# Projections of the first stage: modulation and sample products in four strips, modulation between the projection blocks

## The reference, cut to what matters

```python
mod = (silu(c) @ w_ada + b_ada).reshape(b, 6, d)      # c: 1 prompt row, 8 sample rows; w_ada: 1024 x 6144
sh1, sc1, g1, sh2, sc2, g2 = ...                      # six slices of 1024 columns
hmix = rms_norm(x) * (1.0 + sc1) + sh1
proj = hmix @ w_in                                    # w_in: 1024 x 3072
q, k, v, hc, gb, gc = split(proj)                     # six blocks of 512 columns
q, k = rotary(q), rotary(k)
u = gc * hc ; yconv = gb * conv3(u)                   # gated short convolution
```

## Time and profile before

| | |
|---|---|
| executions | 1468.34, 1470.19, 1476.89 us |
| the profiled execution: time | 1473.47 us |
| its span in the trace | 1471.6 us |
| mean granted clock of TensorE | 0.923 |
| TensorE busy | 1329.9 us (90%) |
| VectorE, ScalarE, GpSimd busy | 463.1, 204.7, 146.4 us |
| DMA | 354.26 MB, mean 241 GB/s |

### The profile page before, as it was taken

One profiled execution on the slowest core, in us unless ns is written; L12 is line 12 of the kernel. 1 busy time (PEld: TensorE's weight loads), 2 busy tenths in 40 slices (PEclk: granted clock), 3 DMA queues, 4 the chain that ended last, 5 costly groups with the idle time before them and its releaser, 6 DMA issues. The chain is left out here.

```text
span 1471.6 us, 19665 instructions
## 1 busy us (share of the span) xinstructions
PE 1329.9 (90%) x5999; PEld 576.9 (39%) x5999; DVE 463.1 (31%) x1185; ACT 204.7 (14%) x410; POOL 146.4 (10%) x152
## 2 busy tenths in 40 slices
PE   4999999988996669988999999899999999899495
PEld 1225554436674424443333333333333333333132
DVE  0340313203333224466233332233233233233248
ACT  0000010003222111111111111111111111111100
POOL 1000000000000010010111111111111111111121
PEclk9999999995558789999999999999999999999868
DMA  9990210019305875004999799989989779967375
GB/s 322 381 318 23 67 49 0 0 41 296 99 0 152 249 250 202 29 4 199 357 382 370 291 372 421 421 307 381 369 340 405 297 307 405 378 246 276 99 312 212
DMA packets 75065, 354.26 MB, mean 241 GB/s; under 512 B 11595, under 2 KB 11595, under 8 KB 44823
## 3 DMA queue, kind: packets, MB, share of 16 engines
q1 hardware_dynamic: 57166, 308.90, 55.8%
q0 software_dynamic: 15680, 37.05, 6.6%
q10 hardware_dynamic: 2130, 7.39, 1.4%
HBM read 338.54 MB, written 34.21 MB: 253 GB/s over the span
## 5 line engine op out<-in xcount | busy, mean ns | idle before, releaser
L1001 PE MATMUL psum<-sb_stream,sb_convg 128*64 128x512 f32 x1664 | 376.8, 606 | 22.7 <-DMA sb_stream<-w_exp_up 21.2
L1001 PEld LDWEIGHTS psum<-sb_stream,sb_convg 128*64 128x64 f32 x1664 | 120.1, 140 | 235.8 <-issue 234.4
L1027 PE MATMUL psum<-sb_stream,sb_aT 128*64 128x512 f32 x832 | 190.0, 598 | 0.0
L1132 POOL DMA_INDIRECT expert_rows<-sb_attn,sb_row x52 | 52.2, 1005 | 542.2 <-DVE sb_token L961 285.0
L500 PE MATMUL psum<-sb_stream,sb_hT 128*128 128x512 f32 (+1 forms) x240 | 105.5, 600 | 0.0
L472 PE MATMUL psum<-sb_hT,sb_stream 128*128 128x512 f32 x192 | 103.9, 634 | 0.6 <-DVE sb_hT L359 0.6
L439 PE MATMUL psum<-sb_stream,sb_cT 128*9 128x512 f32 x192 | 85.3, 608 | 11.5 <-DMA sb_stream<-w_ada 11.5
L1419 DVE TENSOR_TENSOR sb_aT<-psum,sb_aT 128x256 f32<-128x256 f32 x53 | 22.5, 425 | 228.7 <-ACT sb_aT L1205 228.7
L1027 PEld LDWEIGHTS psum<-sb_stream,sb_aT 128*64 128x64 f32 x832 | 55.1, 136 | 95.4 <-issue 89.3
L1447 DVE TENSOR_SCALAR sb_attn<-psum,sb_now_gate 128x512 f32<-128x512 f32 x52 | 39.0, 751 | 148.9 <-PE psum L1027 148.9
L1205 ACT ACTIVATE sb_aT<-psum 128x256 f32<-128x256 f32 x53 | 20.3, 383 | 388.1 <-PE psum L1001 386.7
(11 more groups left out here) (271 smaller groups left out, 1221.8 us busy)
## 6 DMA issues: line engine op xcount, KB each, us to landing
sb_stream<-w_exp_gate SPq DMA_DIRECT2D x65, 1024.0 KB, 7.3
sb_stream<-w_exp_up SPq DMA_DIRECT2D x65, 1024.0 KB, 10.3
sb_stream<-w_exp_down SPq DMA_DIRECT2D x65, 1024.0 KB, 10.3
sb_stream<-w_ada SPq DMA_DIRECT2D x12, 2048.0 KB, 11.9
sb_stream<-expert_rows SPq DMA_DIRECT2D x8, 2048.0 KB, 13.0
sb_stream<-w_in SPq DMA_DIRECT2D x6, 2048.0 KB, 7.9
sb_stream<-cache_k SPq DMA_DIRECT2D x8, 1024.0 KB, 18.5
sb_stream<-cache_v SPq DMA_DIRECT2D x8, 1024.0 KB, 13.3
```

The costliest lines, as they stand in the source:

```text
L1001: last = pe.matmul(psum[lo:lo + LANE, 0, :].rearrange("p (a n) -> p a n", a=2), xT[:, k, lo:lo + LANE], gu[j][:, k, :, :], start=(k == 0), ...
L1027: last = pe.matmul(psum[lo:lo + LANE, 4 + n, :], hidT[:, k, lo:lo + LANE], dn[j][:, k, n * 512:(n + 1) * 512], start=(k == 0), stop=(k == 1))
L1132: pool.indirect_dma_start(expert_rows, bass.IndirectOffsetOnAxis(ap=row[:, u, :], axis=0), out[:, u, :], None, bounds_check=last_expert_ro ...
```

## The change

- **Modulation in strips.** silu(c) is filled up to 32 columns with zeros. A piece of w_ada is now a *slab*: 256 rows of the contraction by 2048 columns (2 MB). Its 8 matmuls write four strips of 32 partitions of one bank: strip j has columns 512j to 512j+511 of the slab. Twelve slabs, four for each third of w_ada; each third has a bank of its own, in which its sums build up. The first third is shift and scale.
- **Order.** Only slabs 0 to 3 stand ahead of the projections; 4 to 6 stand behind the first convolution block, 7 to 9 behind the second, 10 and 11 behind the third. SyncE loads x first, then slabs 0 to 3, three blocks of w_in and so on; slabs and blocks have rings of three slots each.
- **Shift and scale on turned rows.** ScalarE only multiplies x by its norm (`normalize`); TensorE turns x; then scale and shift, turned too by four transposes, are applied to `hT`, where they are one number for each partition: four pieces by VectorE, four by ScalarE. The trip of shift and scale through DRAM is gone.
- **Sample rows in four strips of the contraction.** The 32 sample rows are stationary (128 x 32), 512 columns of w_in move, and the eight pieces of the contraction are spread over four strips, two in each. ScalarE copies the four partial sums out of PSUM, and a matmul with a matrix of four identities under each other (`fold`) adds them up: turned (4 matmuls) for the convolution blocks, as rows (1 matmul) for q, k, v. VectorE's convolution of the sample rows takes all four column tiles at once.

The core of the diff:

```diff
-        bc_shift = tmp("bc_shift", [P, 2, D])
-        bc_scale = tmp("bc_scale", [P, 2, D])
...
+        mod = tmp("mod", [P, 3, W])
+        modT = tmp("modT", [P, 2, KC, 1 + DEC_B])
+        part = tmp("part", [P, W])
+        side = tmp("side", [P, 2, W])
+        product = tmp("product", [P, WC, NS])
...
+        slots = stream[:, :].rearrange("p (s n) -> p s n", s=6)
+        slab = slots[:, 0:3, :].rearrange("p s (k n) -> p s k n", k=2)
+        ring = slots[:, 3:6, :].rearrange("p s (k n) -> p s k n", k=KC)
...
+        ada_bank = (1, 2, 7)
...
+                def load_slab(n):
+                    if n >= 3:
+                        sp.wait_ge(slab_used, n - 2)
+                    s, u = n // 4, n % 4
+                    src = io["w_ada"][0][2 * u * P:2 * (u + 1) * P, s * 4 * W:(s + 1) * 4 * W]
+                    sp.dma_start(slab[:, n % 3], src.rearrange("(k p) n -> p k n", p=P)).then_inc(slab_in[n % 3], 16)
+                def load_block(j):
+                    if j >= 3:
+                        sp.wait_ge(cmm, WC * (j - 2))
+                    src = io["w_in"][0][:, order[j] * W:(order[j] + 1) * W]
+                    sp.dma_start(ring[:, j % 3], src.rearrange("(k p) n -> p k n", p=P)).then_inc(w_in[j % 3], 16)
...
+                sp.dma_start(xh[:, 0:NPT, :], io["x_prompt"][0].rearrange("(t p) n -> p t n", p=P)).then_inc(x_in, 16)
+                sp.dma_start(xh[0:NS, NPT, :], io["x_sample"].rearrange("b t n -> (b t) n")).then_inc(x_in, 16)
+                for n in range(4):
+                    load_slab(n)
+                for j in range(3):
+                    load_block(j)
+                for n in range(4, 8):
+                    load_slab(n)
+                load_block(3)
+                for n in range(8, 11):
+                    load_slab(n)
+                load_block(4)
+                load_slab(11)
+                load_block(5)
...
+                def normalize(t):
+                    r = rows(t)
+                    act.activation(xh[0:r, t, :], xh[0:r, t, :], ACT.Copy, scale=ss[0:r, 0, t:t + 1]).then_inc(h_ok, 1)
...
+                act.wait_ge(mt_ok, 1)
+                for k in range(1, KC, 2):
+                    act.activation(hT[:, k, 0:SEQ], hT[:, k, 0:SEQ], ACT.Identity, bias=modT[:, 0, k, 0:1],
+                                   scale=modT[:, 1, k, 0:1]).then_inc(hT_a, 1)
...
+                    act.wait_ge(part_ps, j + 1)
+                    if j:
+                        act.wait_ge(merged, j)
+                    act.copy(part[:, :], psum[:, 5, :]).then_inc(part_ok, 1)
...
+                take_hc(0)
+                take_part(0)
+                take_hc(1)
+                act.wait_ge(merged, 1)
+                act.copy(hcT[:, :, SEQ:], psum[:, 6, 0:WC * NS].rearrange("p (c n) -> p c n", c=WC)).then_inc(merge_read, 1)
+                take_hc(2)
+                take_hc(3)
+                take_part(1)
+                keep_mod(1)
+                take_part(2)
...
+                def add_bias(s):
+                    v.wait_ge(slab_used, 4 * s + 4)
+                    v.tensor_tensor(mod[:, s, :], psum[:, ada_bank[s], :], mod[:, s, :], ALU.add).then_inc(mod_ok, 1)
...
+                def modulate(k):
+                    v.tensor_scalar(hT[:, k, 0:SEQ], hT[:, k, 0:SEQ], modT[:, 1, k, 0:1], modT[:, 0, k, 0:1],
+                                    ALU.mult, ALU.add).then_inc(hT_v, 1)
...
+                step(v.tensor_tensor(us[:, :, :, 2:], merge, hcs, ALU.mult))
...
-                for n in range(NADA):
-                    pe.wait_ge(w_in[n % 4], 16 * (n // 4 + 1))
-                    if n >= 2:
-                        pe.wait_ge(mod_ok, n - 1)
-                    for k in range(KC):
-                        last = pe.matmul(psum[0:9, 1 + n % 2, :], cT[:, k, :], ring[:, n % 4, k, :],
-                                         start=(k == 0), stop=(k == KC - 1))
-                    last.then_inc(w_used, 1)
...
+                def modulation(slabs):
+                    for n in slabs:
+                        s, u = n // 4, n % 4
+                        pe.wait_ge(slab_in[n % 3], 16 * (n // 3 + 1))
+                        for k in (2 * u, 2 * u + 1):
+                            for j in range(4):
+                                last = pe.matmul(psum[32 * j:32 * (j + 1), ada_bank[s], :], cT[:, k, :],
+                                                 slab[:, n % 3, k % 2, j * W:(j + 1) * W], start=(k == 0), stop=(k == KC - 1))
+                        last.then_inc(slab_used, 1)
...
+                def sample_strips(j):
+                    if j:
+                        pe.wait_ge(part_ok, j)
+                    else:
+                        pe.wait_ge(hT_v, NT + KC // 2 + 1)
+                    for i in range(2):
+                        for a in range(4):
+                            k = 2 * a + i
+                            last = pe.matmul(psum[32 * a:32 * (a + 1), 5, :], hT[:, k, SEQ:], ring[:, j % 3, k, :],
+                                             start=(i == 0), stop=(i == 1))
+                    last.then_inc(part_ps, 1)
...
+                def merge_turned(j):
+                    pe.wait_ge(part_ok, j + 1)
+                    if j:
+                        pe.wait_ge(merge_read, j)
+                    for c in range(WC):
+                        last = pe.matmul(psum[:, 6, c * NS:(c + 1) * NS], part[:, c * P:(c + 1) * P], fold, start=True, stop=True)
+                    last.then_inc(merged, 1)
...
+                    pe.matmul(psum[0:NS, 6, :], fold, part[:, :], start=True, stop=True).then_inc(merged, 1)
...
+                def conv_block(j):
+                    pe.wait_ge(w_in[j % 3], 16 * (j // 3 + 1))
+                    for m in range(WC):
+                        i = j * WC + m
+                        if i >= 2:
+                            if i - 2 < WC:
+                                pe.wait_ge(hc_ok, i - 1)
+                            else:
+                                pe.wait_ge(gcb_ok, i - 1 - WC)
+                        for k in range(KC):
+                            if i == 0:
+                                pe.wait_ge((hT_v, hT_a)[k % 2], NT + k // 2 + 1)
+                            last = pe.matmul(psum[:, 3 + i % 2, :], ring[:, j % 3, k, m * P:(m + 1) * P], hT[:, k, 0:SEQ],
+                                             start=(k == 0), stop=(k == KC - 1))
+                        last.then_inc(cmm, 1)
+                        if m == 0:
+                            sample_strips(j)
+                        if m == 1:
+                            merge_turned(j)
...
+                modulation((0, 1))
...
+                modulation((2, 3))
+                pe.wait_ge(small_in, 7 * 16)
+                for m in range(WC):
+                    last = pe.transpose(psum[:, 7, 16 * m:16 * m + 16], state[:, m * P:(m + 1) * P], ident[0:16, 0:16])
+                last.then_inc(turned, 1)
+                pe.wait_ge(mod_ok, 1)
+                for c in range(4):
+                    last = pe.transpose(psum[:, 0, c * P:(c + 1) * P], mod[:, 0, c * P:(c + 1) * P], ident)
+                last.then_inc(turned, 1)
+                conv_block(0)
+                modulation((4, 5, 6))
+                conv_block(1)
+                modulation((7,))
+                pe.wait_ge(st_ok, 1)
+                modulation((8, 9))
+                conv_block(2)
+                modulation((10, 11))
...
-                            last = pe.matmul(psum[:, 5 + i % 2, 0:NS], ring[:, n % 4, k, m * P:(m + 1) * P], hT[:, k, SEQ:],
-                                             start=(k == 0), stop=(k == KC - 1))
...
+                            last = pe.matmul(psum[:, i % 3, :], hT[:, k, t * P:(t + 1) * P], ring[:, n % 3, k, :],
                                              start=(k == 0), stop=(k == KC - 1))
                         last.then_inc(proj, 1)
+                        if t == 0:
+                            sample_strips(n)
+                        if t == 1:
+                            merge_rows(n)
```

More of the change, by code:

```diff
@@ L234, in _ @@
                 sp.dma_start(cst[:, :], io["cst"]).then_inc(cst_in, 16)
[L235 to L244, removed]
+                sp.dma_start(xh[:, 0:NPT, :], io["x_prompt"][0].rearrange("(t p) n -> p t n", p=P)).then_inc(x_in, 16)
[12 more added lines that the diff above has]
+                load_block(5)
+                sp.wait_ge(qk_ok, 2 * NPT)
                 sp.wait_ge(v_ok, NT)
+                sp.wait_ge(merge_read, 5)
                 for name, src in (("k", k_sb), ("v", v_sb)):
@@ L300, in _, with take_v @@
                     act.activation(convg[:, m, :], convT[:, m, :], ACT.Copy, scale=gains[:, 1, m:m + 1]).then_inc(sq_ok, 1)
-                act.wait_ge(pads, 1)
-                for t in range(NT):
-                    act.wait_ge(proj, 2 * NT + t + 1)
-                    act.copy(v_sb[0:rows(t), t, :], psum[0:rows(t), (2 * NT + t) % 3, :]).then_inc(v_ok, 1)
```

(42 more changed lines are left out.)

262 lines of the change are left out of this document (129 added, 133 removed).

## The result

Four executions of the changed kernel took 1399.79 to 1407.87 us, median 1402.12, beside four of the kernel before with a median of 1469.99: ratio 0.9536 (95% interval 0.9491 to 0.958). Two later series of six against eleven gave 0.9492 (0.9451 to 0.9533) and 0.9517 (0.9487 to 0.9547). The kernel is about 5% faster. The forecast was 1391 (1377 to 1409).

The account below looks back on a forecast made before the run. TensorE's count of matmuls was taken to bound stage 1; head 46 us plus the work behind it gave 247.5 against 326.2, 78.7 less, so 1391 us from the median 1470.19, range 1377 to 1409.

Parts of the forecast that it names:

- Head: Stage 1 up to the first projection: 43.5 us, plus 2.5 for a first 5 us at half clock, 46 together.
- Strips: Stage 1 matmuls on TensorE: four strips of 32 columns run in the time of one, 0.858 us a round.
- return: TensorE going from strips back to the full array in stage 1: 0.15 us each time.
- Cover: Stage 1 behind the first projection: VectorE, ScalarE and load waits cost nothing, hidden behind TensorE's tiles; some 27 us of load slack.
- rivals on the clock: Clock falls to half behind the first projection: about 1592 us, 3 in 100. Stage 2 gets better clock: 1346 to 1376, 4.
- strips that don't overlap: Stage 1: strips don't run beside each other, a round costs 3.43 us, the kernel takes 1475; 3 in 100.
- the tiles: Stage 1 projections: 12 tiles of the convolution and 12 of q, k, v at 6.87 us, 164.9 us, unchanged.
- the upper bound: Whole kernel at 1406 us: 6.5 more before the first projection, 5.9 for rounds at 1.07, 2 for entries into strips.
- folds and slabs: Stage 1 behind the first projection: folds 2.6 and 3.0 us; slabs 4 to 11, 16 rounds and five returns, 14.5.
- the sums of squares: Stage 1, with the tail ahead of k: 4.15 and 0.5 us, as before.
- what is passed on: Stages 2 to 4 behind the barrier: as long as before, so stage 1's saving of 78.7 us is passed on whole.
- The base: Whole kernel: the saving was taken from the median before, 1470.19 us; the profiled execution took 1473.47.

Follow-up runs that it names:

- c0_changed: The changed kernel timed again without any edit, beside the kernel before: median 1401.01 us against 1475.11, ratio 0.9492.
- the early stores: Changed kernel, but SyncE stores the convolution's state and k as soon as ready, only v's stores behind v's last copy: median 1401.74 us against 1404.8, ratio 0.9505.

## Why the prediction was right, and where it was short

The mechanism was right in each of its parts, and experiments show the two large ones.

- *Head.* Forecast 43.5 and 2.5 for a slow start; measured 42.91 and 1.8 (a tile of 8.64, at 0.50 for its first 2 us). In this profile it is bound by w_in, as worked out: the last wait ahead of the first projection is 2.77 us for it. In `c0_changed` the chain behind slab 3 was last and the slow start was missing (43.04 and a tile of 7.04). That the forecast's sum hits the first case is in part luck, worth some 1.5 us.
- *Strips.* 1.86 us for two rounds (1.87 forecast), 5.28 for six (5.3). By the Trainium skill ("TensorE: Matmul & The Clock Gate", Part 3), with its 3.07 times for four strips of rows, a round would have been 1.12 us. The trace has 0.86 and a return of 0.14, so the measurement decides for the full four here.
- *Cover.* No gap between 43 and 249 us: slab 7, block 3 and the folds were never late. The rivals on the clock (granted 0.99 and 0.98 behind the head) and on strips that don't overlap are out by the rows above.
- *Mis-sized: the tiles.* 24 tiles at 6.87 were to be 164.9 us. They took 171.1, of which 1.8 belong to the head. Next to a change of mode a tile is 6.97 to 7.07, which makes some 2.5 us, a price of entering strips that I had only in the upper bound (0.3 of it is the way from the last matmul to the copy of v). The other 1.9 are k's first tile at 8.77 behind the one-column matmuls: the granted clock was 1.00 during these and 0.60 behind them. It was so before (0.50): from the first matmul of that tile to its rotation 263.37 - 254.81 = 8.56 us, where q's first tile at full clock has 222.81 - 215.66 = 7.15, and my 6.87 left that out. On the other side folds and slabs were 0.6 too much, half of it since I counted five returns behind slabs where the list has three, and the sums of squares 0.3. The stage ended at 249.6, not 247.5.
- *Mis-sized: what is passed on.* 76.4 us at the start of stage 2 are 73.7 at the end. I had costed the stages behind at nothing. Of the 2.7 us 1.6 stand ahead of stage 4, as told above, and the other 1.1 are what is left of larger differences of both signs in stages 2 and 3 (the prompt's scores 1.4 us shorter, the stretch behind them 2.2 longer). The cause stays open, and scatter of single profiles can explain it.
- *The base.* I carried the saving over to a median of three runs, 1470.19. With 26 runs of before over three series the median is 1475.1, and 1403.1 for 16 of the changed kernel: 72 us of gain, which agrees with the traces' 73.7. The first series alone says 68. Some 5 of the 11 us by which the forecast missed are this; 5 more are the two points above (78.7 us forecast, 73.7 in the traces).

## What to carry to other kernels

A float32 matmul of 512 columns cost 0.86 us here with 32 stationary columns as with 128, so look for groups with few of them and give each a strip: four of 32 columns ran in the time of one, as long as neighbours in the list went to different strips or came two by two. When a group gets four times cheaper, ask at once whether its weights arrive four times faster; here 28 us of the gain hung on moving it between work that needs no transfers. And what a stage saves at a barrier is only kept if the next stage's first wait is no later: the early stores made the barrier 4.8 us shorter, the masks took 2.5 us back, and the times can't tell what is left of it.

## What the runs showed of the hardware

- TensorE runs strips beside each other over a short stretch of its list only: 2 matmuls in a row for the same strip cost nothing (5.34 us for 24), 6 in a row 15.65 us, with two of each six beside two of the next.
- The 40 one-column matmuls ran at a granted clock of 1.00 (181.7 to 185.6 us), and the tile behind them started at 0.60. Before the change it was 0.93 and 0.50. It cost 1.9 us for a tile that TensorE entered without a gap.
- Transfers with 8 KB rows (slabs) ran at 422 GB/s, those with 2 KB rows (blocks of w_in) at 389, in the same trace and with nothing else to speak of beside them:

```profile
18.00:33.00 15.00, 9.11 (x61) 4.24 (x62) 7.53 (x15) 5.95 (x8) 1.58 (x2) 1.00 1.01 422
37.00:52.00 15.00, 11.70 (x44) 4.76 (x40) 3.87 (x10) 3.27 (x5) 0.00 (x0) 0.89 1.05 389
54.00:60.00 6.00, 6.00 (x16) 2.65 (x15) 0.00 (x0) 0.13 (x1) 0.00 (x0) 1.00 1.00 416
```

  From 54 us on slabs move again, at 416. w_ada itself, in blocks of 512 columns, came at 385 GB/s before, so its bytes cost 8 to 9% less time in slabs. Whether the length of the rows is the reason wasn't tried by itself.
